# Feed-forward weight sums of a seven-product block scheme: all four on VectorE, instead of two on GpSimd and two on VectorE

## The chip, the cores and the metric

One core of a Trainium2 chip runs the whole program. The metric is the device time of one execution, in microseconds (us). The kernel before was timed three times: 1071.74 us median, 1071.22 lowest, 1071.80 highest. The profile is of one more execution, with a time of 1071.1 us of its own.

## What is computed

A trunk of two layers works on 512 tokens of width 1024, all in float32. Each layer adds a token mixer (layer 0: a short gated convolution; layer 1: multi-head latent attention) and then a gated feed-forward block, each on a root-mean-square norm of the running sum `x`. A last norm follows. The change touches the feed-forward block alone:

```
def swiglu_ffn(h, w_gate, w_up, w_down):
    return (jax.nn.silu(h @ w_gate) * (h @ w_up)) @ w_down

# in each of the two layers:
h = rms_norm(x, norm_ffn_g[i])
x = x + swiglu_ffn(h, ffn_w_gate[i], ffn_w_up[i], ffn_w_down[i])   # hidden width 2816
```

## The kernel before, in words

**Two-part numbers.** TensorE multiplies rounded float32 (fp32r). Each operand is split into a high part, a rounded copy, and a low part, the rest; a product is then three matmuls: high by high, high by low, low by high (`product`, lines 430 to 433). The high part is a copy on ScalarE (line 569 for feed-forward weights), the low part a subtraction on VectorE (line 575).

**Half-groups.** The hidden width of 2816 is cut into 11 pairs of 256 columns (`PAIRS_F`). For each pair the gate half comes first (`par` 0) and the up half second (`par` 1), so each layer has 22 half-groups, numbered 0 to 21 here. A half-group multiplies a weight block of 1024 x 256 by the 512 tokens. It does this as a 2 x 2 block product with seven multiplications in place of eight (`OPS` = 7). Each is 4 chunks of 3 matmuls, so a half-group is 84 matmuls of 128 x 256. The seven left operands of a half-group are three blocks of the weights as they are and four sums of them, each 128 x 512 here:

- sum 0 = A21 + A22
- sum 1 = sum 0 - A11
- sum 2 = A11 - A21 (`third_sum`, line 1142)
- sum 3 = A12 - sum 1 (`fourth_sum`, line 1148)

Before the change, GpSimd makes sums 0 and 1 (`weight_sums`, lines 699 and 704) and VectorE makes sums 2 and 3, all into the one buffer `w_sum`. The raw blocks lie in `pair_raw`, one half for gate and one for up, loaded by the SyncE queue (`load_group`, line 603).

**Parts.** The seven operands are split in four parts, high on ScalarE (`make_op_hi`) and then low on VectorE (`make_op_lo`): part 0 is A11 (128 x 512), part 1 is the sums 0 to 2 (128 x 1536), part 2 is sum 3 (128 x 512), part 3 is two raw blocks (128 x 1024). TensorE's product 0 needs part 0. The products 1 to 3 need part 1. Product 4 needs all four parts. The buffers `op_w_hi` and `op_w_lo` hold one set of seven, so that an operand of the next half-group is written as soon as the product of the present one that used it has been counted.

**The order on each engine** is written out by hand, in loops over pairs (pairs 1 to 9; pairs 0 and 10 stand apart). While TensorE works on half-group g, VectorE (`group`, line 1227) does this, `nxt` being g + 1:

```
weights(0)        # low part 0 of nxt
third_sum, fourth_sum of nxt
u_2 = ps + s1     # lines 1258 to 1266, of g
weights(1)        # low part 1 of nxt
w_u3 = ps + u_2   # line 1269, of g
weights(2)        # low part 2 of nxt
c12, c0/c1        # lines 1278 and 1279, of g, after its product 6
weights(3)        # low part 3 of nxt
multiply          # line 1289 (up) or 1292 (gate), of g
```

ScalarE (`group`, line 839) copies `s1` out of PSUM (line 845), makes high part 0, for an up half the silu (line 851), and the high parts 1, 2 and 3. High part 1 waits for `sum_done` (sums 0 and 1) and for `sum_ve` (sum 2). GpSimd makes sum 0 of half-group X as soon as low part 1 of X - 1 is done (the sums are then read for the last time) and its block has landed, then sum 1. The load of half-group X waits on SyncE's queue until low part 3 of X - 2 is done. The first half-group's sums 0 and 1 are made apart, long before the feed-forward phase starts. Those of half-group 1 wait for `x_op_done`, that is for the last step that prepares the token operands. After half-group 21, VectorE turns to the low parts of the down projection's weights (`unit_lo`, line 415) and of the hidden values (`hidden_lo`, line 1222), which TensorE then needs in order.

Of the kernel before, what the change touches and what calls it, by code (L numbers as in the profile page):

```python
# [35 lines left out]
ALU = mybir.AluOpType  # L36
# [6 lines left out]
OPS = 7  # L43
# [48 lines left out]
def trunk_kernel(nc, w, consts, out):  # L92
# [38 lines left out]
    with ExitStack() as ctx:  # L131
# [50 lines left out]
        w_sum, _, e = place("w_sum", [P, 4, S], F32, TMP)  # L182
# [59 lines left out]
        def sem(name):  # L242
            return ctx.enter_context(nc.semaphore(name))
# [16 lines left out]
        xg_new, t_new, x_op_split, x_op_done = sem("xg_new"), sem("t_new"), sem("x_op_split"), sem("x_op_done")  # L260
        pair_in = [sem("pair_in_gate"), sem("pair_in_up")]
        sum_done, sum_ve, op_hi, op_lo, op_used = sem("sum_done"), sem("sum_ve"), sem("op_hi"), sem("op_lo"), sem("op_used")
# [20 lines left out]
        def wait(eng, semaphore, value):  # L283

            if isinstance(value, int) and value <= 0:
                return
            eng.wait_ge(semaphore, value)
# [191 lines left out]
        def squares_before(n):  # L479

            return X_POOL + (n - 1) * DC if n else 0
# [37 lines left out]
        PAIRS_F = FC // 2  # L519

        def group_no(l, i, par):

            return i * 2 + (2 * PAIRS_F * l + par)

        def op_no(l, i, par, p):

            return i * (2 * OPS) + (2 * OPS * PAIRS_F * l + OPS * par + p)

        def after(l, i, par):

            if par == 0:
                return l, i, 1
            return l, i + 1, 0

        def blocks(par):

            even, odd = pair_raw[:, par, 0:DC:2, :], pair_raw[:, par, 1:DC:2, :]
            return {"A11": even[:, :, P:2 * P], "A12": odd[:, :, P:2 * P],
                    "A21": even[:, :, 0:P], "A22": odd[:, :, 0:P]}

        def wide(part, n):
            return part[:, n, :].rearrange("p (c m) -> p c m", m=P)
# [116 lines left out]
        @block.gpsimd  # L659
        def _(pool):  # L660
            nc.gpsimd.memset(mean[:, :], 1.0 / D).then_inc(mean_set, 1)
            nc.gpsimd.memset(small[:, :], EPS).then_inc(mean_set, 1)
            nc.gpsimd.memset(z[:, 0:2], 0.0).then_inc(z_pad, 1)

            def load_gains(row, g):
                n = g.shape[0]
                pool.dma_start(gain_rows[row:row + n, :], g).then_inc(gain_in, 16)

            load_gains(rows["ffn0"], w["norm_ffn_g"].rearrange("l (r c) -> (l r) c", c=P))
            load_gains(rows["final"], w["final_norm_g"].rearrange("(r c) -> r c", c=P))  # L670
            load_gains(rows["tap0"], w["conv_w"].rearrange("a t (r c) -> (a t r) c", c=P))
            load_gains(rows["q_norm"], w["mla_q_norm_g"].rearrange("a (r c) -> (a r) c", c=P))
            load_gains(rows["kv_norm"], w["mla_kv_norm_g"].rearrange("a (r c) -> (a r) c", c=P))

            def clear_sum(n):
                if n:
                    pool.wait_ge(stat_done, ROOT[n])
                nc.gpsimd.memset(sq_sum[:, :], 0.0).then_inc(sq_zero, 1)

            def add_square(n, m, ready, count):  # L680

                wait(pool, ready, count)
                wait(pool, sq_added, m + squares_before(n))
                nc.gpsimd.tensor_tensor(sq[:, :], xT[:, ds(m, 1), :].rearrange("p a s -> p (a s)"),
                                        xT[:, ds(m, 1), :].rearrange("p a s -> p (a s)"), ALU.mult).then_inc(sq_new, 1)
                wait(pool, sq_new, m + (squares_before(n) + 1 - n // 2))
                pool.wait_ge(sq_zero, n // 2 + 1)
                nc.gpsimd.tensor_tensor(sq_sum[:, :], sq_sum[:, :], sq[:, :], ALU.add).then_inc(sq_added, 1)

            def weight_sums(l, i, par):  # L690

                b = blocks(par)
                done = i * 4 + (4 * PAIRS_F * l + 2 * par)
                free = op_no(l, i, par, 0) - OPS
                wait(pool, pair_in[par], i * 16 + 16 * (PAIRS_F * l + 1))
                if not isinstance(free, int) or free >= 0:
                    wait(pool, op_lo, free + 4)
                    wait(pool, sum_done, done)
                nc.gpsimd.tensor_tensor(wide(w_sum, 0), b["A21"], b["A22"], ALU.add).then_inc(sum_done, 1)  # L699
                if not isinstance(free, int) or free >= 0:  # L700
                    wait(pool, op_lo, free + 4)
                    wait(pool, sum_ve, done)
                wait(pool, sum_done, done + 1)
                nc.gpsimd.tensor_tensor(wide(w_sum, 1), wide(w_sum, 0), b["A11"], ALU.subtract).then_inc(sum_done, 1)

            def ffn(l):

                pool.wait_ge(x_op_done, 12 * (l + 1))
                weight_sums(l, 0, 1)

                with pool.Fori(1, PAIRS_F) as i:
                    for par in range(2):
                        weight_sums(l, i, par)

            clear_sum(0)
            for m in range(X_POOL):
                add_square(0, m, x_copied, m + 1)
            def normalise(hd):

                par = hd % 2  # L720
                for n, js in enumerate(((3, 1), (2, 0))):
                    pool.wait_ge(rec_done, 2 * hd + n + 1)
                    for j in js:
                        blk = prob[:, par, L_OFF[j]:L_OFF[j] + (j + 1) * P]
                        ins = nc.gpsimd.tensor_scalar(blk, blk, rec[:, par, j:j + 1], 1.0, ALU.mult, ALU.mult)  # L725
                ins.then_inc(p_ready, 1)

            for n, name in ((1, "conv_out"), (2, "down0"), (3, "mla_out"), (4, "down1")):
                if n == 3:
                    for hd in range(HEADS):  # L730
                        normalise(hd)
                if n % 2:
                    weight_sums(n // 2, 0, 0)
                    ffn(n // 2)
                else:
                    if n == 4:
                        pool.wait_ge(op_used, op_no(1, PAIRS_F - 1, 1, OPS))
                        pool.dma_start(gain_row[:, :], w["final_norm_g"][D - LW:D].unsqueeze(0).broadcast_to([P, LW])
                                       ).then_inc(gain_row_in, 16)
                    clear_sum(n)  # L740
                    with pool.Fori(0, DC - 2 * (n == 4)) as m:
                        add_square(n, m, tile_free, m + (T0[name] + 1))
                if n == 2:
                    latents(pool)
# [319 lines left out]
        def _(ve):  # L1064
# [69 lines left out]
                conv_body(i)  # L1134
            conv_body(DC - 1)

            def third_sum(l, i, par):

                b = blocks(par)
                wait(ve, pair_in[par], i * 16 + 16 * (PAIRS_F * l + 1))  # L1140
                wait(ve, op_lo, op_no(l, i, par, 0) - OPS + 4)
                nc.vector.tensor_tensor(wide(w_sum, 2), b["A11"], b["A21"], ALU.subtract).then_inc(sum_ve, 1)  # L1142
# [74 lines left out]
            def ffn(l, n_inv):  # L1217
# [9 lines left out]
                def group(i, par, first=False, last=False):  # L1227

                    g, op0 = group_no(l, i, par), op_no(l, i, par, 0)
                    nxt = None if last and par else after(l, i, par)  # L1230
                    b0 = 4 * par
                    pair = hid[:, ds(i * 2, 2), :].rearrange("p a (h n) -> p (a h) n", h=2)
                    to = pair if par else gate

                    def weights(part):
                        if nxt is not None:
                            make_op_lo(ve, *nxt, part)
                        elif part < 3:
                            unit_lo(ve, f"down{l}", 0, part)

                    early = first and par == 0
                    if early:
                        third_sum(*nxt)
                    weights(0)
                    if nxt is not None:
                        if not early:
# [24 lines left out]
                    if nxt is None:  # L1271
                        for q in range(3, 6):
                            hidden_lo(q)
                    else:
                        weights(2)
                    wait(ve, op_used, op0 + 7)
                    wait(ve, w_u3_done, g + 1)
                    nc.vector.tensor_tensor(to[:, 2, :], ps[:, b0 + 3, N:S], w_u3[:, 0, :], ALU.add).then_inc(c12_done, 1)
# [1 line left out]
                                            w_u3[:, 1, :].unsqueeze(1).broadcast_to([P, 2, N]),  # L1280
                                            ALU.add).then_inc(set_read, 1)
                    weights(3)
                    if first and par == 0:
                        ve.wait_ge(inv_ready, n_inv + 1)
                    wait(ve, c12_done, g + 1)
# [674 lines left out]
```

## Time and profile before, and how to read it

| | |
|---|---|
| median of the three timed executions | 1071.74 us |
| the profiled execution's own time | 1071.1 us |
| its span | 1069.3 us |
| TensorE's granted clock | 0.999 of full |
| TensorE busy | 1059.4 us (99%) |
| VectorE busy | 804.0 us (75%) |
| ScalarE busy | 478.4 us (45%) |
| GpSimd busy | 225.0 us (21%) |
| chain that ended last | TensorE 96%, VectorE 2%, DMA 1% |
| sums on GpSimd, lines 699 and 704 | 44 each |

The engines are PE (TensorE matmul), PEld (its weight loads), DVE (VectorE), ACT (ScalarE), POOL (GpSimd) and SPq (SyncE's queue). In the timeline a row is one instruction: start and duration in us from the start of the span, engine, line, operation, what it writes and reads, its shape, and in brackets how long the engine sat idle before it and what ended that. Instructions on one engine overlap a little: the start of the next can lie before the end of this one, so the price of an instruction in a full queue is the distance between two starts, not its duration. In the waits, a row tells who waited for whom, how long in total, how often and at most.

### The profile page before, as it was taken

The page shows a single profiled execution, that of the slowest core. Times are in us where ns is not written, and L with a number is a line of the kernel's source. Part 1 is how long each engine was busy: PE and PEld are TensorE (multiplying, and loading weights), DVE is VectorE, ACT ScalarE, POOL GpSimd, SP SyncE. Part 2 cuts the span into 40 slices and gives each one's busy share as a digit, 9 for nine tenths or more (in the row PEclk, how much of TensorE's full clock was granted, in tenths as well). Part 3 has the DMA queues.
Part 4 walks back from the last instruction along what each step waited for, and adds up shares of the span by engine and source line. Part 5 has one row for each costly group of instructions (what it writes and reads, how often), then busy time and mean ns, then how long its engine had stood idle before and what let it go on. Part 6 is the DMA issues. An engine that isn't in the chain of part 4 may idle for free.

```text
span 1069.3 us, 18448 instructions
## 1 busy us (share of the span) xinstructions
PE 1059.4 (99%) x6654; PEld 944.4 (88%) x6654; DVE 804.0 (75%) x1108; ACT 478.4 (45%) x715; POOL 225.0 (21%) x211
## 2 busy tenths in 40 slices
PE   8999999999999999999999999999999999999997
PEld 7888888999999998888878766789999999988897
DVE  5755659999999999544455687599999999975453
ACT  6312236644444546222346777465444444552222
POOL 6000001323323320122110355013332332202010
PEclk9999999999999999999999999999999999999999
DMA  7334242232332332432436511113323323342311
GB/s 201 107 90 117 78 119 79 80 119 82 115 118 81 115 108 79 139 94 81 125 99 144 136 49 47 41 40 119 99 98 118 98 98 118 100 118 85 114 61 79
DMA packets 144008, 106.54 MB, mean 100 GB/s; under 512 B 4488, under 2 KB 140096, under 8 KB 143968
## 3 DMA queue, kind: packets, MB, share of 16 engines
q1 hardware_dynamic: 143392, 104.80, 32.7%
q0 software_dynamic: 544, 1.21, 0.4%
q8 instruction: 23, 0.38, 0.1%
q14 instruction: 17, 0.14, 0.0%
q10 hardware_dynamic: 32, 0.01, 0.0%
HBM read 99.72 MB, written 2.10 MB: 95 GB/s over the span
## 4 chain that ended last, share of the span: by engine, by line
PE 96%; DVE 2%; DMA 1%; issue 0%; ACT 0%; POOL 0%; SPq 0%; DVEq 0%; ACTq 0%
PE ps L431 29%; PE ps L432 29%; PE ps L433 29%; PE ps L1744 3%; PE ps L1805 2%; PE ps L1821 2%; DMA x_nat<-in_x 1%; DVE op_w_lo L575 1%; PE ps L1788 0%; PE ps L1786 0%; PE ps L1787 0%; DVE w_sum L1142 0%; PE ps L490 0%; POOL prob L725 0%; PE ps L1878 0%
## 5 line engine op out<-in xcount | busy, mean ns | idle before, releaser
L431 PE MATMUL ps<-x_op_hi,op_w_hi 128*128 128x256 f32 x1232 | 349.1, 283 | 0.7 <-DVE op_w_lo L575 0.7
L432 PE MATMUL ps<-x_op_lo,op_w_hi 128*128 128x256 f32 x1232 | 348.6, 283 | 0.0
L433 PE MATMUL ps<-x_op_hi,op_w_lo 128*128 128x256 f32 x1232 | 348.6, 283 | 0.0
L431 PEld LDWEIGHTS ps<-x_op_hi,op_w_hi 128*128 128x128 f32 x1232 | 236.5, 192 | 2.4 <-issue 1.1
L432 PEld LDWEIGHTS ps<-x_op_lo,op_w_hi 128*128 128x128 f32 x1232 | 236.5, 192 | 0.1
L433 PEld LDWEIGHTS ps<-x_op_hi,op_w_lo 128*128 128x128 f32 x1232 | 236.5, 192 | 0.0
L415 DVE TENSOR_TENSOR wgt_lo<-raw,wgt_hi 128x1024 fp32r<-128x1024 f32 (+5 forms) x119 | 127.7, 1089 | 80.3 <-ACT wgt_hi L402 79.3
L431 PE MATMUL ps<-hid_hi,wgt_hi 128*128 128x512 f32 x476 | 186.8, 392 | 0.0
L433 PE MATMUL ps<-hid_hi,wgt_lo 128*128 128x512 f32 x476 | 185.3, 389 | 0.0
L432 PE MATMUL ps<-hid_lo,wgt_hi 128*128 128x512 f32 x476 | 185.3, 389 | 0.0
L402 ACT ACTIVATE wgt_hi<-raw 128x1024 fp32r<-128x1024 f32 (+5 forms) x119 | 99.4, 848 | 142.0 <-PE ps L433 134.7
L699 POOL TENSOR_TENSOR w_sum<-pair_raw 128x512 f32<-128x512 f32 x44 | 59.5, 1353 | 489.2 <-DVE op_w_lo L575 259.3
L575 DVE TENSOR_TENSOR op_w_lo<-w_sum,op_w_hi 128x1536 fp32r<-128x1536 f32 x88 | 139.0, 1579 | 19.3 <-ACT op_w_hi L569 19.2
L569 ACT ACTIVATE op_w_hi<-w_sum 128x1536 fp32r<-128x1536 f32 x88 | 89.5, 1053 | 107.4 <-DVE w_sum L1142 93.9
L431 PEld LDWEIGHTS ps<-hid_hi,wgt_hi 128*128 128x128 f32 x476 | 89.4, 188 | 18.8 <-issue 0.4
L433 PEld LDWEIGHTS ps<-hid_hi,wgt_lo 128*128 128x128 f32 x476 | 89.3, 188 | 18.8
L432 PEld LDWEIGHTS ps<-hid_lo,wgt_hi 128*128 128x128 f32 x476 | 89.4, 188 | 18.2 <-issue 0.2
L575 DVE TENSOR_TENSOR op_w_lo<-pair_raw,op_w_hi 128x512 fp32r<-128x512 f32 x88 | 92.3, 1049 | 0.0
L431 PE MATMUL ps<-xg_hi,wgt_hi 128*128 128x512 f32 x232 | 92.0, 396 | 0.0
L433 PE MATMUL ps<-xg_hi,wgt_lo 128*128 128x512 f32 x232 | 90.4, 390 | 0.0
L432 PE MATMUL ps<-xg_lo,wgt_hi 128*128 128x512 f32 x232 | 90.3, 389 | 0.0
L569 ACT ACTIVATE op_w_hi<-pair_raw 128x512 fp32r<-128x512 f32 x88 | 74.0, 841 | 25.7 <-issue 13.8
(186 smaller groups left out, 1355.2 us busy)
## 6 DMA issues: line engine op xcount, KB each, us to landing
pair_raw<-in_ffn_w_gate SPq DMA_DIRECT2D x22, 1024.0 KB, 5.2
pair_raw<-in_ffn_w_up SPq DMA_DIRECT2D x22, 1024.0 KB, 5.2
raw<-in_conv_w_in SPq DMA_DIRECT2D x24, 512.0 KB, 3.8
raw<-in_ffn_w_down SPq DMA_DIRECT2D x28, 384.0 KB, 3.3
raw<-in_ffn_w_down SPq DMA_DIRECT2D x28, 320.0 KB, 3.0
raw<-in_conv_w_out SPq DMA_DIRECT2D x8, 512.0 KB, 3.7
raw<-in_mla_w_o SPq DMA_DIRECT2D x8, 512.0 KB, 3.9
raw<-in_ffn_w_down SPq DMA_DIRECT2D x5, 512.0 KB, 4.9
```

What stands on the lines that cost most here:

```text
L402: ins = nc.scalar.activation(dst, src, ACT.Copy)
L415: ins = nc.vector.tensor_tensor(dst, src, hi.bitcast(F32), ALU.subtract)
L431: nc.tensor.matmul(acc, wh, xh, start=first, stop=False)
L432: nc.tensor.matmul(acc, wh, xl, start=False, stop=False)
L433: return nc.tensor.matmul(acc, wl, xh, start=False, stop=last)
L569: nc.scalar.activation(four(op_w_hi[:, slots, :]), src, ACT.Copy).then_inc(op_hi, PART_SIZE[part])
L575: nc.vector.tensor_tensor(four(op_w_lo[:, slots, :]), src, four(op_w_hi[:, slots, :]).bitcast(F32), ALU.subtract).then_inc(op_lo, PART_SIZ ...
L699: nc.gpsimd.tensor_tensor(wide(w_sum, 0), b["A21"], b["A22"], ALU.add).then_inc(sum_done, 1)
L1744: ins = nc.tensor.matmul(ps[:, bank, col:col + W], q_Ts[hd % 2][:, hd // 2, j * P:(j + 1) * P], k_T[:, hd, 0:W], start=True, stop=True)
L1805: ins = nc.tensor.transpose(ps[:, bank, col + (j - b) * P:col + (j - b + 1) * P], prob[:, hd % 2, L_OFF[j] + b * P:L_OFF[j] + (b + 1) * P] ...
L1821: ins = nc.tensor.matmul(ps[VD * par:VD * par + VD, 6 + pair % 2, b * P:S], v_nat[:, b, hd * VD:(hd + 1) * VD], prob_Ts[par][:, 0, PT_OFF[ ...
```

## The change

The loop over half-groups on GpSimd goes; of `weight_sums` what is left makes the sums 0 and 1 of each layer's first half-group (gate half of pair 0). VectorE makes sums 0 and 1 of half-group 1 in `first_sums`, around its `third_sum`, in front of low part 0. Those of half-groups 2 to 21 are made two half-groups ahead: in VectorE's `group` of g, `sum_0` of g + 2 stands behind low part 2 of g + 1 and `sum_1` of g + 2 behind low part 3 of g + 1.

```diff
@@ gpsimd
-            def weight_sums(l, i, par):
-
-                b = blocks(par)
-                done = i * 4 + (4 * PAIRS_F * l + 2 * par)
-                free = op_no(l, i, par, 0) - OPS
-                wait(pool, pair_in[par], i * 16 + 16 * (PAIRS_F * l + 1))
-                if not isinstance(free, int) or free >= 0:
-                    wait(pool, op_lo, free + 4)
-                    wait(pool, sum_done, done)
+            def weight_sums(l):
+
+                b = blocks(0)
+                done = 4 * PAIRS_F * l
+                pool.wait_ge(pair_in[0], 16 * (PAIRS_F * l + 1))
+                if l:
+                    pool.wait_ge(op_lo, op_no(l, 0, 0, 0))
+                    pool.wait_ge(sum_ve, done)
                 nc.gpsimd.tensor_tensor(wide(w_sum, 0), b["A21"], b["A22"], ALU.add).then_inc(sum_done, 1)
-                if not isinstance(free, int) or free >= 0:
-                    wait(pool, op_lo, free + 4)
-                    wait(pool, sum_ve, done)
-                wait(pool, sum_done, done + 1)
+                pool.wait_ge(sum_done, done + 1)
                 nc.gpsimd.tensor_tensor(wide(w_sum, 1), wide(w_sum, 0), b["A11"], ALU.subtract).then_inc(sum_done, 1)
-
-            def ffn(l):
-
-                pool.wait_ge(x_op_done, 12 * (l + 1))
-                weight_sums(l, 0, 1)
-
-                with pool.Fori(1, PAIRS_F) as i:
-                    for par in range(2):
-                        weight_sums(l, i, par)
...
                 if n % 2:
-                    weight_sums(n // 2, 0, 0)
-                    ffn(n // 2)
+                    weight_sums(n // 2)
@@ vector
+            def first_sums(l):
+
+                b = blocks(1)
+                done = 4 * PAIRS_F * l + 2
+                ve.wait_ge(pair_in[1], 16 * (PAIRS_F * l + 1))
+                ve.wait_ge(op_lo, op_no(l, 0, 1, 0) - OPS + 4)
+                ve.wait_ge(sum_done, done)
+                nc.vector.tensor_tensor(wide(w_sum, 0), b["A21"], b["A22"], ALU.add).then_inc(sum_done, 1)
+                third_sum(l, 0, 1)
+                ve.wait_ge(sum_done, done + 1)
+                nc.vector.tensor_tensor(wide(w_sum, 1), wide(w_sum, 0), b["A11"], ALU.subtract).then_inc(sum_done, 1)
+
+            def sum_0(l, i, par):
+
+                b = blocks(par)
+                wait(ve, pair_in[par], i * 16 + 16 * (PAIRS_F * l + 1))
+                wait(ve, op_lo, op_no(l, i, par, 0) - OPS + 4)
+                nc.vector.tensor_tensor(wide(w_sum, 0), b["A21"], b["A22"], ALU.add).then_inc(sum_done, 1)
+
+            def sum_1(l, i, par):
+
+                wait(ve, sum_done, i * 4 + (4 * PAIRS_F * l + 2 * par + 1))
+                wait(ve, sum_ve, i * 4 + (4 * PAIRS_F * l + 2 * par))
+                nc.vector.tensor_tensor(wide(w_sum, 1), wide(w_sum, 0), blocks(par)["A11"], ALU.subtract).then_inc(sum_done, 1)
...
                     nxt = None if last and par else after(l, i, par)
+                    then = None if last else after(*nxt)
...
                     if early:
-                        third_sum(*nxt)
+                        first_sums(l)
                     weights(0)
...
                     else:
                         weights(2)
+                    if then is not None:
+                        sum_0(*then)
                     wait(ve, op_used, op0 + 7)
...
                     weights(3)
+                    if then is not None:
+                        sum_1(*then)
```

## Rows read from the trace of the kernel before

**Rows 1.** The page's first part: busy time, share, instructions of each engine.
```profile
PE 1059.4 (99%) x6654; PEld 944.4 (88%) x6654; DVE 804.0 (75%) x1108; ACT 478.4 (45%) x715; POOL 225.0 (21%) x211
```

**Rows 2.** What TensorE waited for from 186 to 1000 us (total, times, longest).
```profile
PE ps L431 <- DVE op_w_lo L575: 0.7, 2, 0.3
```

**Rows 3.** VectorE's timeline over one half-group: start, duration, what it does.
```profile
359.79 1.76 DVE L575 TENSOR_TENSOR op_w_lo<-w_sum,op_w_hi 128x1536 fp32r<-128x1536 f32 x1 [0.48 <-ACT op_w_hi L569]
361.47 0.68 DVE L1269 TENSOR_TENSOR w_u<-ps,gate_u 128x512 f32<-128x512 f32 x1
362.07 1.49 DVE L575 TENSOR_TENSOR op_w_lo<-w_sum,op_w_hi 128x512 fp32r<-128x512 f32 x1
363.48 0.41 DVE L1278 TENSOR_TENSOR gate_u<-ps,w_u 128x256 f32<-128x256 f32 x1
363.82 0.68 DVE L1279 TENSOR_TENSOR gate_u<-ps,w_u 128x512 f32<-128x512 f32 x1
364.41 1.38 DVE L575 TENSOR_TENSOR op_w_lo<-pair_raw,op_w_hi 128x1024 fp32r<-128x1024 f32 x1
365.72 1.21 DVE L1292 TENSOR_TENSOR gate_u<-gate_u,inv 128x1024 f32<-128x1024 f32 x1
366.86 0.68 DVE L575 TENSOR_TENSOR op_w_lo<-pair_raw,op_w_hi 128x512 fp32r<-128x512 f32 x1
367.46 0.68 DVE L1142 TENSOR_TENSOR w_sum<-pair_raw 128x512 f32<-128x512 f32 x1
368.06 0.68 DVE L1148 TENSOR_TENSOR w_sum<-pair_raw,w_sum 128x512 f32<-128x512 f32 x1
368.66 0.68 DVE L1262 TENSOR_TENSOR hid<-ps,s 128x512 f32 x1
369.82 1.76 DVE L575 TENSOR_TENSOR op_w_lo<-w_sum,op_w_hi 128x1536 fp32r<-128x1536 f32 x1 [0.48 <-ACT op_w_hi L569]
```

**Rows 4.** ScalarE's and GpSimd's timelines, 361 to 373 us.
```profile
362.44 0.38 ACT L845 ACTIVATE s<-ps 128x256 f32<-128x256 f32 x1 [0.41 <-PE ps L433]
368.23 2.01 ACT L569 ACTIVATE op_w_hi<-w_sum 128x1536 fp32r<-128x1536 f32 x2 [0.20 <-DVE w_sum L1142]
372.52 0.38 ACT L845 ACTIVATE s<-ps 128x256 f32<-128x256 f32 x1 [0.41 <-PE ps L433]
361.71 1.29 POOL L699 TENSOR_TENSOR w_sum<-pair_raw 128x512 f32<-128x512 f32 x1 [7.03 <-DVE op_w_lo L575]
363.08 1.63 POOL L704 TENSOR_TENSOR w_sum<-w_sum,pair_raw 128x512 f32<-128x512 f32 x1
```

**Rows 5.** VectorE's timeline late in layer 1, where GpSimd is idle.
```profile
928.84 0.68 DVE L575 TENSOR_TENSOR op_w_lo<-w_sum,op_w_hi 128x512 fp32r<-128x512 f32 x1
930.37 1.22 DVE L575 TENSOR_TENSOR op_w_lo<-pair_raw,op_w_hi 128x1024 fp32r<-128x1024 f32 x1
```

**Rows 6.** The load of the weight blocks: an issue, and times to landing.
```profile
365.95 0.37 SPq L603 DMA_DIRECT2D pair_raw<-in_ffn_w_up  x1
DMA to landing us min/median/max: 5.0/5.2/6.3
```

**Rows 7.** Timelines of the start of the feed-forward phases.
```profile
194.16 1.77 DVE L1142 TENSOR_TENSOR w_sum<-pair_raw 128x512 f32<-128x512 f32 x1
198.84 1.76 DVE L575 TENSOR_TENSOR op_w_lo<-w_sum,op_w_hi 128x1536 fp32r<-128x1536 f32 x1
197.25 2.01 ACT L569 ACTIVATE op_w_hi<-w_sum 128x1536 fp32r<-128x1536 f32 x2 [1.21 <-POOL w_sum L704]
200.66 0.19 PEld L431 LDWEIGHTS ps<-x_op_hi,op_w_hi 128*128 128x128 f32 x1 [0.54 <-DVE op_w_lo L575]
725.90 1.76 DVE L575 TENSOR_TENSOR op_w_lo<-w_sum,op_w_hi 128x1536 fp32r<-128x1536 f32 x1
```

**Rows 8.** Timelines of the end of layer 0's half-groups and the down projection.
```profile
399.93 1.76 DVE L575 TENSOR_TENSOR op_w_lo<-w_sum,op_w_hi 128x1536 fp32r<-128x1536 f32 x1 [0.51 <-ACT op_w_hi L569]
419.30 0.19 PEld L431 LDWEIGHTS ps<-hid_hi,wgt_hi 128*128 128x128 f32 x1 [0.26 <-DVE wgt_lo L415]
```

## The prediction, on record before the changed kernel was run

> **What bounds the kernel now.** First the busy shares [rows 1]: TensorE is busy for 99% of the span, so the kernel is bound by it, and almost nothing can be won. TensorE's waits in the two feed-forward phases and after say the same: it waited for VectorE 0.7 us in all, twice [rows 2]. VectorE's 75% is a mean over phases and hides what counts here. So the third view is VectorE's timeline over one half-group of the steady part [rows 3]. Eleven instructions stand back to back, from one low part 1 at 359.79 to the next at 369.82, a cycle of 10.03 us, with one gap of 0.48 in it. TensorE's cycle is read from ScalarE's copy of `s1`, which TensorE's first product releases: 372.52 - 362.44 = 10.08 us [rows 4]. So VectorE, 95% full, is only 0.05 us per half-group faster than TensorE. Whatever is added to its cycle, net of what is taken off, must fit in 0.05 us or TensorE waits.
>
> **What the gap is.** It looks like room, and the question is whether the new sums can use it. It ends when ScalarE has made high part 1. That conversion starts when sum 2 is done (its releaser is line 1142 [rows 4]), and low part 1 waits for it. From the start of sum 2 (367.46) to the start of low part 1 (369.82) there are thus 2.36 us: the sum 0.68, the hand-over 0.09 (ScalarE starts at 368.23), the conversion and the hand-over back 1.59 (the row's 2.01 are two conversions in one). In that time VectorE does sum 3 and the `u_2` addition, and then idles. Sum 0 and sum 1 are put elsewhere in the cycle, behind low parts 2 and 3. The 2.36 us stay, gap included.
>
> **What is added.** Two sums of 128 x 512. The nearest rows are sums 2 and 3: same shape, same buffers, each 0.68 long but 0.60 apart from the next start [rows 3]. So 2 x 0.60 = 1.20 us per half-group. The upper bound is 2 x 0.68 = 1.36, if nothing overlaps. I take 0.60, since each new sum stands between neighbours that don't need its result at once, as the old ones do. A new sum also brings two more waits on VectorE's queue; they are for its own finished work and, for sum 0, for the weight block.
>
> The Trainium skill ("VectorE: DVE Perf Modes", the section on the TRN2 errata) gives a float32 tensor_tensor of N elements as (N + 151)/0.96 ns, so 691 ns at 512. Taken as the price of each sum, it would lift the cycle worked out below by another 0.18 us and the total by about 7 us. The rows have 0.68 as duration but 0.60 as distance; I go by the distance.
>
> **What is taken off.** Two of VectorE's instructions are slowed while GpSimd works. GpSimd's sums run 361.71 to 363.00 and 363.08 to 364.71 [rows 4]. Low part 2, started at 362.07, lasts 1.49 and the next starts 1.41 later; low part 3, started at 364.41, lasts 1.38, next after 1.31 [rows 3]. Where GpSimd is idle the same two last 0.68 and 1.22 [rows 5], which in a full queue means distances of 0.60 and 1.14 (those of the 0.68 and 1.21 rows in rows 3). Refund: 0.81 + 0.17 = 0.98 us. The instructions that read PSUM beside GpSimd (0.68, 0.41, 0.68) are not longer than elsewhere, so nothing comes back there. GpSimd's own work and its waits cost nothing now: nobody but ScalarE at the start of a layer waits for it.
>
> **The new cycle**, from low part 1 to low part 1: 1.68 (low 1) + 0.60 (`w_u3`) + 0.60 (low 2) + 0.60 (sum 0) + 0.34 (c12) + 0.59 (c0/c1) + 1.14 (low 3) + 0.60 (sum 1) + 1.14 (multiply) + 0.60 (low 0) + 2.36 = **10.25 us**. Check with the old pieces: 10.03 - 0.98 + 1.20 = 10.25. That is 0.17 above TensorE's 10.08. TensorE can start product 1 when low part 1 is done, so it falls to VectorE's pace.
>
> **Is anything else late first?** Measured from the start of low part 1: TensorE's product 1 starts at 1.82 (200.66 - 198.84 [rows 7]) when it waits. Product 4 follows three products of 1.44 later (10.08/7), at 6.14; low part 3 then ends at 4.41 + 1.22 = 5.63, so 0.5 us in hand. The load of a block is issued 0.16 after low part 3 (365.95 [rows 6] against 364.41 + 1.38), so at 5.79, and lands at 11.0, at the slowest 12.1. Sum 0 needs it at 10.25 + 2.88 = 13.1. It is now VectorE's queue that would stand, where GpSimd's did, but there is 1.0 to 2.1 us in hand. Both are hidden; if that cover went, each late load would cost its lateness once.
>
> **The start of each layer** gets better. Now, sum 2 of half-group 1 lasts 1.77 beside GpSimd, ScalarE is kept 1.21 us by GpSimd's sum 1, and TensorE's weight load waits 0.54 us at 200.66 [rows 7]. After: sum 0 at 194.16, sum 2 at 194.76, sum 1 at 195.36, done 196.04, just when ScalarE comes free (197.25 - 1.21). The hand-over of 0.09 and the 1.59 bring low part 1 to about 197.8, in place of 198.84. TensorE could start product 1 at 197.8 + 1.82 = 199.6 and wants it at 200.66 - 0.54 = 200.1: no wait, 0.5 us in hand, eaten after three half-groups at 0.17 each.
>
> **The sum.** Low part 1 is made for half-groups 1 to 21, 20 cycles between them, each with both new sums. TensorE's product 1 of half-group 21: now 200.66 + 20 x 10.08 = 402.3; after, 199.62 + 20 x 10.25 = 404.6. So +2.36 us in layer 0, and the same in layer 1, whose start repeats it (725.90 [rows 7]). Then the down projection: VectorE works on without a gap, and the load of the second weight slice already waits 0.26 us for it at 419.30 [rows 8]. VectorE is now 402.26 - 399.93 = 2.33 us ahead of TensorE's product 1, after the change 1.82, so this wait grows by 0.5 in layer 0 and appears in layer 1. I put 0.6 for each layer, an estimate. In all 2 x (2.36 + 0.6) = +5.9 us. On the profiled execution's 1071.1 that makes 1077.0. The median is 0.6 higher; I put the forecast between, at **1077.3**.
>
> **The rivals.**
> - *The gap takes the sums in.* If the 0.48 us were free time, the cycle would be 9.77 us, below 10.08, and TensorE would stay the bound. Place: between sum 2 and low part 1; it decides once the cycle is at or under 10.08, so if the 2.36 us shrank by 0.17. For it: the page shows VectorE with idle time, and refund and gap together (1.46) exceed 1.20. Against it: the gap is the tail of a hand-over through ScalarE. Then only the start waits (2 x 0.54) and the 0.26 come back: 1.3 us less than 1071.1, so 1069.8. Chance 0.14, of it 0.03 on the far side of 0.2%.
> - *Dearer sums.* Each at 0.68 or a little more, because the added waits uncover them or because they don't overlap: 0.08 x 2 x 20 x 2 = 6.4 us more, about 1083.5. Against it: sum 3 and the `u_2` addition also have waits and still stand 0.60 apart. Chance 0.10.
> - *A late block.* A load more than 2.1 us slower than the median holds up VectorE, a microsecond or so each time: 1078 to 1081. The slowest of all landed in 6.3, against 5.2, so it is unlikely. Chance 0.03.
> - That the change does not do what it says can be left out: the loop over half-groups is gone from GpSimd's program.
>
> **How the numbers follow.** The forecast has 0.73. Its own bounds: were the cycle 0.08 us shorter (a hand-over a little shorter, or the refund a little larger), 20 x 2 x 0.08 = 3.2 us less, 1074; with half of the dearer sums' price, 3.2 to 4 more, 1081. The range of 1074.0 to 1081.5 takes in the forecast, the late block and part of the dearer sums, about 0.8. About 0.2% (2.1 us) is what a measurement of this kernel can tell from no change. Slower: 0.73 + 0.10 + 0.03 = 0.86. Same: 0.11. Faster: 0.03.
>
> **What the changed profile would show.** VectorE's low part 1 rows 10.25 us apart in the steady part; low part 2 at 0.68 and low part 3 at 1.22; the two new sums 0.60 from the next start; the gap of 0.48 before low part 1 still there. TensorE waiting for low part 1 some 17 times per layer at about 0.17 us, and `s1` copies 10.25 apart. The first low part 1 near 197.8 with no wait of TensorE at that place. I am wrong if the low part 1 rows stay 10.08 or less apart, if the gap has shrunk, or if TensorE waits for something other than low part 1, such as low part 3 or a weight block.

## Result and profile after

The changed kernel takes 1077.60 us (median of 6, 1077.12 to 1078.67) against 1071.48 us for the kernel before in the same comparison (6 runs, 1071.06 to 1071.91). The ratio is 1.0059, 95% interval 1.0049 to 1.0069: 6.1 us slower. The forecast was 1077.3 us, with a range of 1074.0 to 1081.5. Two single executions among all the comparisons, 1302.3 us of the kernel before and 5351.1 us of one experiment, lie far outside the others and are left out of the ratios.

The page of the changed kernel, first part and the engines' line of the chain of waits:

```profile
PE 1066.4 (99%) x6654; PEld 947.4 (88%) x6654; DVE 810.5 (75%) x1192; ACT 477.5 (44%) x715; POOL 99.9 (9%) x127
...
PE 11%; DVE 0%; ACT 0%; issue 0%; DVEq 0%; ACTq 0%
```

The first line answers to [rows 1]. GpSimd has lost 84 instructions and 125 us, and VectorE has gained the 84 instructions. But VectorE's busy time has risen by 6.5 us only, where 84 sums at 0.60 each (a sum's step in a full queue) are 50 us: most of what it took over it got back, because its own instructions are no longer held up. By this line TensorE is as much the bound as before. The chain is of no help here: the part that the view follows back covers 11% of the span and begins in the last down projection.

VectorE's timeline over one half-group of the changed kernel, the counterpart of [rows 3]:

```profile
361.89 1.76 DVE L575 TENSOR_TENSOR op_w_lo<-w_sum,op_w_hi 128x1536 fp32r<-128x1536 f32 x1 [0.48 <-ACT op_w_hi L569]
363.57 0.69 DVE L1281 TENSOR_TENSOR w_u<-ps,gate_u 128x512 f32<-128x512 f32 x1
364.17 0.68 DVE L575 TENSOR_TENSOR op_w_lo<-w_sum,op_w_hi 128x512 fp32r<-128x512 f32 x1
364.77 0.69 DVE L1140 TENSOR_TENSOR w_sum<-pair_raw 128x512 f32<-128x512 f32 x1
365.37 0.42 DVE L1292 TENSOR_TENSOR gate_u<-ps,w_u 128x256 f32<-128x256 f32 x1
365.70 0.68 DVE L1293 TENSOR_TENSOR gate_u<-ps,w_u 128x512 f32<-128x512 f32 x1
366.30 1.22 DVE L575 TENSOR_TENSOR op_w_lo<-pair_raw,op_w_hi 128x1024 fp32r<-128x1024 f32 x1
367.44 0.69 DVE L1146 TENSOR_TENSOR w_sum<-w_sum,pair_raw 128x512 f32<-128x512 f32 x1
368.04 1.22 DVE L1308 TENSOR_TENSOR gate_u<-gate_u,inv 128x1024 f32<-128x1024 f32 x1
369.17 0.69 DVE L575 TENSOR_TENSOR op_w_lo<-pair_raw,op_w_hi 128x512 fp32r<-128x512 f32 x1
369.77 0.69 DVE L1153 TENSOR_TENSOR w_sum<-pair_raw 128x512 f32<-128x512 f32 x1
370.38 0.68 DVE L1159 TENSOR_TENSOR w_sum<-pair_raw,w_sum 128x512 f32<-128x512 f32 x1
370.98 0.68 DVE L1274 TENSOR_TENSOR hid<-ps,s 128x512 f32 x1
372.14 1.76 DVE L575 TENSOR_TENSOR op_w_lo<-w_sum,op_w_hi 128x1536 fp32r<-128x1536 f32 x1 [0.48 <-ACT op_w_hi L569]
```

The reader is to see four things. The new sums (lines 1140 and 1146) stand 0.60 before the next start. Low part 2 lasts 0.68 and low part 3 lasts 1.22, where they were 1.49 and 1.38. The gap of 0.48 in front of low part 1 is still there. And from one low part 1 to the next it is 10.25 us in place of 10.03; all 40 distances of this kind in the two layers lie between 10.25 and 10.28.

TensorE's rows where half-group 17 asks for its low part 1, done at 363.65 (weight loads, then the matmul):

```profile
363.40 0.19 PEld L433 LDWEIGHTS ps<-x_op_hi,op_w_lo 128*128 128x128 f32 x1
363.70 0.19 PEld L431 LDWEIGHTS ps<-x_op_hi,op_w_hi 128*128 128x128 f32 x1
...
363.71 0.39 PE L431 MATMUL ps<-x_op_hi,op_w_hi 128*128 128x256 f32 x1
```

In the steady part weight loads are otherwise 0.12 apart. Here it is 0.30. A step of this kind, in 17 half-groups of each layer, is most of the loss; the down projections add to it, and the better start takes something off. It is so small that neither the idle times in brackets nor the list of waits names it. One finds it by comparing distances. A longer one is listed: in the experiment below with the extra instruction outside the gap, the same wait stands in the list 38 times, with 0.5 us at most.

### The profile page after: what moved, and what is told of

Same layout as the page of the kernel before. It is cut to its first block and busy times, and to the rows that moved or that the text cites. A ratio compares the mean times of both kernels' runs of the same rounds, so it can differ in the third digit from the quotient of the medians.

```text
span 1075.4 us, 18337 instructions
## 1 busy us (share of the span) xinstructions
PE 1066.4 (99%) x6654; PEld 947.4 (88%) x6654; DVE 810.5 (75%) x1192; ACT 477.5 (44%) x715; POOL 99.9 (9%) x127
## 3 DMA queue, kind: packets, MB, share of 16 engines
q0 software_dynamic: 544, 1.21, 0.4%
## 5 line engine op out<-in xcount | busy, mean ns | idle before, releaser
L575 DVE TENSOR_TENSOR op_w_lo<-w_sum,op_w_hi 128x1536 fp32r<-128x1536 f32 x88 | 107.4, 1220 | 19.3 <-ACT op_w_hi L569 19.3
L575 DVE TENSOR_TENSOR op_w_lo<-pair_raw,op_w_hi 128x512 fp32r<-128x512 f32 x88 | 83.6, 950 | 0.0
L837 ACT ACTIVATE gate_u<-gate_u 128x1024 f32<-128x1024 f32 x20 | 21.2, 1061 | 85.4 <-DVE gate_u L1308 85.4
```

The source lines that it names most:

```text
L575: nc.vector.tensor_tensor(four(op_w_lo[:, slots, :]), src, four(op_w_hi[:, slots, :]).bitcast(F32), ALU.subtract).then_inc(op_lo, PART_SIZ ...
L837: nc.scalar.activation(gate, gate, ACT.Silu).then_inc(act_done, 1)
```

## Experiments

The theory is the one of the prediction. VectorE and ScalarE form a loop (sum 2, ScalarE's conversion, low part 1, and round VectorE's queue back to sum 2). Its 10.25 us are above TensorE's 10.08, and the gap in it can't be used where it stands. The rivals: VectorE simply has too much work; the loss is a fixed sum at the start or the end of a layer; the added waits cost. All ratios are to the kernel before on the same chip.

### The start alone

From the kernel before, only half-group 1 of each layer is changed (`first_sums` itself is as in the change and not shown):

```diff
 # gpsimd, ffn(l)
-                pool.wait_ge(x_op_done, 12 * (l + 1))
-                weight_sums(l, 0, 1)
 # vector, group
                     if early:
-                        third_sum(*nxt)
+                        first_sums(l)
```

> Half of the change alone: VectorE makes sums 0 and 1 of half-group 1 of each layer (the start), GpSimd keeps those of half-groups 2 to 21. Theory (VectorE's cycle against TensorE's): VectorE's cycle stays 10.03 us, below TensorE's 10.08, so only the start changes; TensorE's two waits of 0.54 us and the 0.26 at the down projection go: 1.0 to 1.3 us below the kernel before, ratio about 0.9989. Rival (the change costs because work left GpSimd at the start, or because new waits stand on VectorE's queue): at or above the kernel before.

Measured: 1069.59 us against 1071.39, ratio 0.9984 (0.9975 to 0.9994). The low parts 1 stand 10.01 to 10.09 apart, but for the first distance of each layer (10.34) and one more in layer 0 (10.32). The 10.32 has a cause that the kernel before shows too, where the same distance is 10.33. A weight block came late, so GpSimd's sums started late, and its sum 1 met the multiply instead of low part 2. GpSimd and VectorE in the kernel before:

```profile
231.57 1.50 POOL L699 TENSOR_TENSOR w_sum<-pair_raw 128x512 f32<-128x512 f32 x1 [7.72 <-DMA pair_raw<-in_ffn_w_up]
233.15 2.15 POOL L704 TENSOR_TENSOR w_sum<-w_sum,pair_raw 128x512 f32<-128x512 f32 x1
...
234.08 2.31 DVE L1289 TENSOR_TENSOR hid<-hid,gate_u 128x1024 f32 x1
```

The multiply lasts 2.31 in place of 1.21. In the kernel before this made TensorE 0.15 late, once; with the better start it did not reach TensorE. TensorE's waits for low part 1 are gone from the list, and of those for the down projection's weights this is left:

```profile
PEld ps L431 <- DVE wgt_lo L415: 0.2, 1, 0.2
```

This half of the change is a gain, of 1.8 us where 1.0 to 1.3 were expected; the interval (0.6 to 2.7 us) takes in both. Work leaving GpSimd at the start is not what costs.

### The loop alone

From the changed kernel, the two sums of half-group 1 go back to GpSimd (the call of `start_sums` is not shown):

```diff
 # gpsimd
+            def start_sums(l):
+                b = blocks(1)
+                ...
+                nc.gpsimd.tensor_tensor(wide(w_sum, 0), b["A21"], b["A22"], ALU.add).then_inc(sum_done, 1)
+                ...
+                nc.gpsimd.tensor_tensor(wide(w_sum, 1), wide(w_sum, 0), b["A11"], ALU.subtract).then_inc(sum_done, 1)
 # vector, group
                     if early:
-                        first_sums(l)
+                        third_sum(*nxt)
```

> The other half alone: GpSimd makes sums 0 and 1 of half-group 1, VectorE those of half-groups 2 to 21. Theory: the first low part 1 comes at 198.84 as in the kernel before, 0.98 us later than in the changed kernel, and as every later one hangs on it 10.25 us apart, all of it reaches the end, in both layers: 2.0 us above the changed kernel, about 1079.6 us, ratio 1.0075. Rival (the loss is a fixed sum, for instance of the start or of the down projection, or TensorE has room to make the delay good): 1077.6 or below.

Measured: 1079.35 us, ratio 1.0073 (1.0058 to 1.0089), 1.75 above the changed kernel. The first low part 1 is at 198.72, where it is at 197.86 in the changed kernel, and all 40 distances are 10.24 to 10.27. The two halves are -1.8 and +8.0 us; their sum of 6.2 is the 6.1 of the whole. A delay of 0.9 us of the loop's first turn is found again at the end of each layer. So the loop is the bound from its first turn to its last, and no fixed sum.

### More work in the gap, and outside it

In both, the changed kernel gets one more instruction of 128 x 256 in each of the 20 half-groups per layer that make sums ahead; nobody reads the result. The place of the buffer `spare` is not shown.

```diff
 # in the gap
+                    if then is not None:
+                        nc.vector.tensor_tensor(spare[:, :].rearrange("p (c m) -> p c m", m=P), blocks(1 - par)["A11"][:, 0:2, :],
+                                                blocks(1 - par)["A21"][:, 0:2, :], ALU.subtract)
                     weights(1)
 # outside it
                     if then is not None:
                         sum_1(*then)
+                        nc.vector.tensor_tensor(spare[:, :].rearrange("p (c m) -> p c m", m=P), blocks(par)["A11"][:, 0:2, :],
+                                                blocks(par)["A21"][:, 0:2, :], ALU.subtract)
```

> The changed kernel with one more subtraction of 128 x 256 (0.41 us long, 0.34 to the next start) into a buffer nobody reads, in each of the half-groups that make sums ahead, between the u_2 addition and low part 1, so inside the gap of 0.48. Theory: it ends 0.1 before the conversion does, the cycle stays 10.25: 1077.6 us, as the changed kernel. Rival (VectorE is bound by the amount of its work): 0.34 x 20 x 2 = 13.6 us more, 1091 us.

> The changed kernel with the same extra subtraction, but behind sum 1 and in front of the multiply, outside the gap. Theory: the cycle is 10.59, all of it reaches the end: 0.34 x 20 x 2 = 13.6 us more, 1091.2 us, ratio 1.0184. Rival (idle time of VectorE takes work in wherever it stands): 1077.6.

Measured in the gap: 1077.79 us, ratio 1.0059 (1.0042 to 1.0075), the changed kernel's time. Measured outside: 1090.45 us, ratio 1.0176 (1.0159 to 1.0193), 12.9 above the changed kernel. VectorE's timeline with the extra instruction in the gap:

```profile
361.63 0.41 DVE L1281 TENSOR_TENSOR spare<-pair_raw 128x256 f32<-128x256 f32 x1
362.20 1.76 DVE L576 TENSOR_TENSOR op_w_lo<-w_sum,op_w_hi 128x1536 fp32r<-128x1536 f32 x1 [0.15 <-ACT op_w_hi L570]
```

and with it outside:

```profile
351.94 0.42 DVE L1300 TENSOR_TENSOR spare<-pair_raw 128x256 f32<-128x256 f32 x1
352.27 1.22 DVE L1311 TENSOR_TENSOR gate_u<-gate_u,inv 128x1024 f32<-128x1024 f32 x1
...
356.38 1.76 DVE L576 TENSOR_TENSOR op_w_lo<-w_sum,op_w_hi 128x1536 fp32r<-128x1536 f32 x1 [0.48 <-ACT op_w_hi L570]
```

The same instruction, the same engine, the same idle time of 0.48 per half-group: free in the one place, 0.34 per half-group in the other. In the gap the idle time shrinks to 0.15 and the distances stay 10.25. Outside, the gap stays and the distances are 10.59. "VectorE simply has too much work" falls by this pair: what counts is the work that stands outside the gap.

### Only sum 0 on VectorE

From the changed kernel, `sum_1` is taken off VectorE's queue. GpSimd makes it in its loop, as soon as sum 0 is there; `sum_0` waits in addition for the half-group before (that wait and GpSimd's loop are not shown).

```diff
 # gpsimd
+            def pool_sum_1(l, i, par):
+                wait(pool, sum_done, i * 4 + (4 * PAIRS_F * l + 2 * par + 1))
+                wait(pool, sum_ve, i * 4 + (4 * PAIRS_F * l + 2 * par))
+                nc.gpsimd.tensor_tensor(wide(w_sum, 1), wide(w_sum, 0), blocks(par)["A11"], ALU.subtract).then_inc(sum_done, 1)
 # vector, group
-                    if then is not None:
-                        sum_1(*then)
```

> In the loop only sum 0 is made on VectorE, behind low part 2; sum 1 goes back to GpSimd, released by sum 0. Theory (what GpSimd costs VectorE is a stop for as long as its sum runs): VectorE saves 0.60, but GpSimd's sum 1 runs from about 3.7 to 5.0 us after the start of low part 1, and low part 3 (two operands in SBUF) starts at 4.41 and is held up by about 0.55: a cycle of about 10.20, so 2 us below the changed kernel, 1075.6 us. The two PSUM readers in between stay at 0.41 and 0.68. Rival (no such stop, or only a small one): a cycle of 9.65 and TensorE as the bound, 1070 us.

Measured: 1070.93 us, ratio 0.9996 (0.9987 to 1.0006). The stop is there, but smaller than expected, and the time is near the rival's. VectorE's low part 3 and GpSimd's sum 1 in two neighbouring half-groups:

```profile
353.12 1.68 DVE L575 TENSOR_TENSOR op_w_lo<-pair_raw,op_w_hi 128x1024 fp32r<-128x1024 f32 x1
...
363.23 1.60 DVE L575 TENSOR_TENSOR op_w_lo<-pair_raw,op_w_hi 128x1024 fp32r<-128x1024 f32 x1
...
352.42 1.29 POOL L706 TENSOR_TENSOR w_sum<-w_sum,pair_raw 128x512 f32<-128x512 f32 x1 [8.82 <-DVE w_sum L1154]
362.46 1.30 POOL L706 TENSOR_TENSOR w_sum<-w_sum,pair_raw 128x512 f32<-128x512 f32 x1 [8.75 <-DVE w_sum L1154]
```

Low part 3 lasts 1.68 or 1.60 in place of 1.22: a stop of 0.46 or 0.38, where 0.55 were put. The cycle is 10.12 in layer 1, and 10.12 and 10.04 by turns in layer 0, where 10.20 were put. At this point 0.08 us of cycle decide: 10.20 would be 0.12 above TensorE and 10.12 is 0.04 above it, and then the lead from the better start lasts for most of the layer: ScalarE's copies of `s1`, which show TensorE's pace, stay 10.08 apart through all of layer 0 and more than half of layer 1. Of the 1.6 us by which the trace is longer than that of the start alone, 0.35 is in the rest of layer 1, and the waits at the down projections are 1.4 in place of 0.2. What was wrong was the size of the stop, not its kind. The alternation in layer 0 goes with GpSimd: sum 1 starts 0.84 us after sum 0 in one half-group and 0.76 in the next, and in layer 1 it is always 0.84. Why it starts earlier at times is left open.

### Sum 2 earlier, first try

In the changed kernel sum 2 of half-group g + 2 is made right behind its sum 1.

```diff
                     if then is not None:
                         sum_1(*then)
+                        third_sum(*then)
 ...
-                        if not early:
-                            third_sum(*nxt)
                         fourth_sum(*nxt)
```

> The changed kernel with sum 2 of half-group g + 2 made right behind its sum 1, in front of the multiply, in place of behind low part 0 a half-group later. VectorE's work is the same, instruction for instruction. Theory (the bound is the loop sum 2, ScalarE's conversion, low part 1, with a gap nobody could use): the conversion now runs under the multiply and low part 0; the gap of 0.48 goes in gate-to-up half-groups, and shrinks to about 0.3 where the silu stands in front of the conversion on ScalarE, so VectorE needs 9.8 and 10.1 us by turns, 9.9 in the mean, under TensorE's 10.08. TensorE is the bound again and the waits at the start stay away: about 1070.0 us, ratio 0.9988 to the kernel before, 7.5 us below the changed kernel. Rival (VectorE simply has too much work, or the added waits cost): 1077.6, as the changed kernel.

Measured: 1071.10 us, ratio 0.9997 (0.9988 to 1.0006). That is 6.5 below the changed kernel with the same work on VectorE, and 1.1 above the expectation. The distances are 9.69 and 10.52 by turns, where 9.8 and 10.1 were put. The half-group with the silu, VectorE and then ScalarE:

```profile
366.34 1.21 DVE L1307 TENSOR_TENSOR gate_u<-gate_u,inv 128x1024 f32<-128x1024 f32 x1
...
370.12 1.76 DVE L575 TENSOR_TENSOR op_w_lo<-w_sum,op_w_hi 128x1536 fp32r<-128x1536 f32 x1 [0.77 <-ACT op_w_hi L569]
...
367.58 1.06 ACT L837 ACTIVATE gate_u<-gate_u 128x1024 f32<-128x1024 f32 x1 [4.51 <-DVE gate_u L1307]
368.55 1.99 ACT L569 ACTIVATE op_w_hi<-w_sum 128x1536 fp32r<-128x1536 f32 x2
```

The conversion starts when the silu is done, and the silu when the multiply is done. Sum 2 in front of the multiply makes all of this 0.60 late. The mean of the two cycles is 10.105, still 0.025 above TensorE's. In the trace it is 209.9 us from a layer's first `s1` copy to its last, where the start alone has 209.45; that is 0.9 us in the two layers, about the miss. Two repairs follow from this reading, and both were run.

### Two repairs

Sum 2 exchanged with low part 0, so that it stands behind the multiply (from the changed kernel):

```diff
                     if early:
                         first_sums(l)
+                    elif nxt is not None:
+                        third_sum(*nxt)
                     weights(0)
                     if nxt is not None:
-                        if not early:
-                            third_sum(*nxt)
                         fourth_sum(*nxt)
```

> The changed kernel with two neighbours on VectorE's queue exchanged: sum 2 stands in front of low part 0, not behind it, and behind the multiply as before. The earlier try had put it in front of the multiply, which made the silu on ScalarE 0.60 late, and the silu stands in front of the conversion. Theory (loop of sum 2, conversion, low part 1, with the silu's chain of multiply, silu, conversion, low part 1 beside it): from the multiply to low part 1 it is 1.14 + 4 x 0.60 = 3.55 us where no silu stands between, so 9.70 for the cycle, and 1.24 + 1.06 + 1.49 = 3.79 with the silu, so 9.94; both under TensorE's 10.08. TensorE is the bound: 1069.6 us, as the kernel with the start alone, ratio 0.9984, 8 us below the changed kernel, with all sums on VectorE. Rival (VectorE's amount of work, or its added waits, keep it behind TensorE): 1071 or more.

Sum 2 as in the first try, with ScalarE's silu behind the conversion of part 1:

```diff
-                    if par:
-                        wait(sc, gate_new, i + (PAIRS_F * l + 1))
-                        nc.scalar.activation(gate, gate, ACT.Silu).then_inc(act_done, 1)
                     for part in range(1, 4):
                         wait(sc, op_used, op0 + USED_BEFORE[part])
                         make_op_hi(sc, *nxt, part)
+                        if par and part == 1:
+                            wait(sc, gate_new, i + (PAIRS_F * l + 1))
+                            nc.scalar.activation(gate, gate, ACT.Silu).then_inc(act_done, 1)
```

> The earlier try (sum 2 in front of the multiply) with ScalarE's silu put behind the conversion of part 1. Theory (in that try the half-groups with a silu took 10.52 us because the silu held the conversion up, and that alone kept it from the full gain): now every cycle is 9.69, TensorE is the bound, 1069.6 us, 1.5 below that try's 1071.1. The silu's result is wanted half a cycle later than it comes, so its new place costs nothing. Rival (the 10.52 come from VectorE's order itself, or the gain is used up by something else): 1071.1 as in that try.

Measured: 1069.55 us, ratio 0.9985 (0.9975 to 0.9994), for the exchange, and 1069.74 us, ratio 0.9987 (0.9978 to 0.9996), for the silu behind. In the exchange the first distances are 9.94 and 9.68, as worked out. After three to four half-groups VectorE is so far ahead that it waits for TensorE. VectorE and ScalarE in that kernel:

```profile
365.74 0.69 DVE L1153 TENSOR_TENSOR w_sum<-pair_raw 128x512 f32<-128x512 f32 x1
366.35 0.69 DVE L575 TENSOR_TENSOR op_w_lo<-pair_raw,op_w_hi 128x512 fp32r<-128x512 f32 x1
...
368.01 0.69 DVE L1274 TENSOR_TENSOR hid<-ps,s 128x512 f32 x1 [0.37 <-PE ps L433]
368.62 1.75 DVE L575 TENSOR_TENSOR op_w_lo<-w_sum,op_w_hi 128x1536 fp32r<-128x1536 f32 x1
...
365.86 1.06 ACT L837 ACTIVATE gate_u<-gate_u 128x1024 f32<-128x1024 f32 x1 [2.86 <-DVE gate_u L1308]
366.83 1.48 ACT L569 ACTIVATE op_w_hi<-w_sum 128x1536 fp32r<-128x1536 f32 x1
```

The gap in front of low part 1 is gone. What idle time VectorE has left is in front of the `u_2` addition, and its releaser is now TensorE: that is how the same engine looks when it is ahead. With the silu behind, ScalarE:

```profile
366.81 1.49 ACT L569 ACTIVATE op_w_hi<-w_sum 128x1536 fp32r<-128x1536 f32 x1 [3.55 <-PE ps L433]
368.20 1.04 ACT L840 ACTIVATE gate_u<-gate_u 128x1024 f32<-128x1024 f32 x1
```

Its first distances are 9.68 and 9.67. The exchange is thus faster than both kernels, by 1.6 and by 8 us, and it is no faster than the start alone (1069.59): once TensorE is the bound, it doesn't matter who makes the sums of the loop.

## Why the prediction was right

- **The price of a sum, 0.60.** Confirmed: lines 1140 and 1146 stand 0.60 to 0.61 before the next start, all 80 times. The added waits cost nothing, and the rival of dearer sums falls. So does the late block: no distance is longer than 10.28.
- **The refund, 0.98.** Confirmed: low parts 2 and 3 last 0.68 and 1.22, with distances of 0.60 and 1.14.
- **The gap stays.** Confirmed in the timeline at 0.48, and tested by the pair of extra instructions. The rival "the gap takes the sums in" is wrong for the place where the change put them, and right for the other place: moving sum 2 instead makes the gap vanish.
- **The cycle, 10.25.** Measured 10.25.
- **The start.** Low part 1 was put at 197.8 and came at 197.86. Alone, the better start brings 1.8 us, not the 1.1 to 1.3 of its terms. The two traces, also 1.8 apart, say where. The waits at the start are 1.2 of it and the late block in layer 0 is 0.15. Another 0.24 arises before the first half-group, where both kernels do the same work, and 0.2 between the layers, in which the shorter down-projection wait has a small share. So the 0.24 is no effect of the start, and most of the 0.2 is not explained.
- **The down projection.** The wait of 0.26 [rows 8] was to grow by 0.5 and to appear in layer 1; 0.6 for each layer was put as an estimate. The list of waits of the changed kernel:

```profile
PEld ps L431 <- DVE wgt_lo L415: 1.8, 2, 0.9
```

  So 0.9 in each layer, 0.6 and 0.9 more than before at the weight load. Past the last half-group the two traces drift apart by 0.5 us in layer 0 and by 0.75 in layer 1. The term was small and about right.
- **The sum.** 5.9 put, 6.1 measured, and not by luck. TensorE's product 1 of half-group 21 was to come 2.36 us later in each layer; in the traces it comes 2.37 later in layer 0 (404.73 against 402.36) and 2.44 in layer 1, counted from each layer's start.
- **What was not as written.** The prediction wanted TensorE's waits for low part 1 seen as some 17 waits per layer. They are there as stretched distances only, 17 between the `s1` copies of each layer, most of them 10.25; the list of waits has none. Had the cycle not been worked out before, the waits view would have cleared VectorE.

The later expectations went wrong twice, by 0.1 to 0.4 us of a cycle: the stop by GpSimd (0.46 or 0.38 and not 0.55), and the silu's chain (10.52 and not 10.1), which the first try with sum 2 moved along without its being counted.

## What to carry to other kernels

Where two engines run the same loop side by side, compare their cycles by the distance from one row to its next turn, not by busy shares or lists of waits: 0.17 us in 10 cost 0.6% here and left no wait behind that the list shows, while 0.5 us did. Idle time of an engine is room only for work that may stand where the idle time is; a gap that ends with another engine's result belongs to a loop, and the cheap remedy is to start that loop's first member earlier, with every chain beside it (here the silu's) worked out as well. Work moved off a slow engine can get a refund from the instructions that it used to hold up, here 0.98 of 1.20 us; read it where the slow engine happens to be idle.

## What the runs showed of the hardware

GpSimd's sum holds up a VectorE instruction that reads two operands in SBUF, and does so almost until it ends. These cases agree. Low part 2 began 0.93 before the end of a GpSimd sum and lost 0.81 [rows 3, 4]. Low part 3 began 0.30 before it and lost 0.17 [rows 3, 4]. The multiply beside the late sum 1 began 1.22 before it (234.08 against 233.15 + 2.15) and lost 1.10. With only sum 0 on VectorE, low part 3 began 0.59 before it (353.12 against 352.42 + 1.29) and lost 0.46, and in the next half-group 0.53 and lost 0.38. So the loss is the overlap less 0.12 to 0.15. GpSimd is held up in turn: its sum 1, which starts while low part 2 is still there, lasts 1.63 [rows 4], and 1.29 where no such instruction is under way. VectorE's instructions with one operand in PSUM, in the same stretches, were not longer (0.41 and 0.68).

The Trainium skill ("SBUF — State Buffer", section "SBUF: two separate sides") says that the port pair of GpSimd and VectorE is an exclusive lock: whichever instruction starts first has it to its end and the other is blocked, and a VectorE operation with two SBUF inputs is one of these, beside a GpSimd operation that reads SBUF. The rows agree, in the order too, but for the tenth of a microsecond at the end. Its formula for a float32 tensor_tensor ("VectorE: DVE Perf Modes", section on the TRN2 errata: 691 ns for 512 elements) fits the duration of 0.68 to 0.69 here. The price in a full queue is 0.60: with the two new sums at the formula's price, an estimate, the cycle would have come out at 10.43 in place of the measured 10.25.
